# Hyena transforms handed over by halves of the frequencies, low parts of turned tiles ahead of the last taps

## The reference

```python
def long_conv(u, k):
    n = 2 * u.shape[1]
    uf = jnp.fft.rfft(u.astype(jnp.float32), n=n, axis=1)
    kf = jnp.fft.rfft(k, n=n, axis=0)
    return jnp.fft.irfft(uf * kf[None], n=n, axis=1)[:, :u.shape[1]].astype(u.dtype)

def hyena_mixer(a, ...):
    u = dwconv_centered(a @ in_w + in_b, conv_w, conv_b)
    x1, x2, v = jnp.split(u, 3, axis=-1)
    z = x1 * (long_conv(v, two_sided(...)) + v * bias[0])
    y = x2 * (long_conv(z, two_sided(...)) + z * bias[1])
    return y @ out_w + out_b
```

## Time and profile before

| | us |
|---|---|
| median of three runs | 2147.05 |
| lowest and highest | 2145.24, 2148.67 |
| the profiled execution | 2147.36 |
| its span, first to last instruction | 2145.5 |
| TensorE busy with matmuls | 2001.8 |
| VectorE busy | 1321.3 |
| ScalarE busy | 686.0 |
| GpSimd busy | 202.8 |

### The profile page before, as it was taken

How to read it: one execution, slowest core, us unless ns; L and a number is a source line. 1 busy time by engine, 2 the same in 40 slices (tenths; PEclk the granted TensorE clock), 3 DMA queues, 4 the chain that set the end, 5 groups by cost and what they waited for, 6 DMA issues and landing times. The chain is left out here.

```text
span 2145.5 us, 24954 instructions
## 1 busy us (share of the span) xinstructions
PE 2001.8 (93%) x10136; PEld 1672.0 (78%) x10136; DVE 1321.3 (62%) x1844; ACT 686.0 (32%) x913; POOL 202.8 (9%) x140
## 2 busy tenths in 40 slices
PE   5899999999989989999999999999899797698998
PEld 2688888878867868888887888888787784398998
DVE  6565546777857675554767565567765548845544
ACT  3422222232200232222224222222444335634442
POOL 1000000100023400000110000011000003340001
PEclk9999999999989999999999999999999898999999
DMA  8444435544520154442645444355432322444554
GB/s 322 152 159 155 137 106 183 165 139 135 179 76 1 41 165 148 139 155 83 201 153 171 138 152 143 104 173 165 147 118 89 118 84 74 123 133 152 186 155 141
DMA packets 274590, 298.25 MB, mean 139 GB/s; under 512 B 8912, under 2 KB 249136, under 8 KB 272688
## 3 DMA queue, kind: packets, MB, share of 16 engines
q1 hardware_dynamic: 270784, 285.44, 41.6%
q10 hardware_dynamic: 3696, 11.27, 1.4%
HBM read 290.31 MB, written 6.37 MB: 138 GB/s over the span
## 5 line engine op out<-in xcount | busy, mean ns | idle before, releaser
L1493 PE MATMUL banks<-xh,wh 128*128 128x512 f32 (+1 forms) x2120 | 782.3, 369 | 53.1 <-DVE xl L946 16.4
L1494 PE MATMUL banks<-xl,wh 128*128 128x512 f32 (+1 forms) x2120 | 777.0, 366 | 0.0
L1495 PE MATMUL banks<-xh,wl 128*128 128x512 f32 (+1 forms) x2120 | 776.4, 366 | 0.0
L883 DVE TENSOR_TENSOR wl<-raw,wh 128x2048 fp32r<-128x2048 f32 (+1 forms) x195 | 404.2, 2073 | 333.0 <-ACT wh L558 331.9
L558 ACT ACTIVATE wh<-raw 128x2048 fp32r<-128x2048 f32 (+1 forms) x201 | 349.6, 1739 | 644.6 <-PE banks L1495 562.9
L1493 PEld LDWEIGHTS banks<-xh,wh 128*128 128x128 f32 x2120 | 408.4, 193 | 124.5 <-issue 27.5
L1494 PEld LDWEIGHTS banks<-xl,wh 128*128 128x128 f32 x2120 | 408.4, 193 | 62.4
L1495 PEld LDWEIGHTS banks<-xh,wl 128*128 128x128 f32 x2120 | 407.8, 192 | 63.1
L1493 PE MATMUL banks<-gh,wh 128*128 128x512 f32 (+1 forms) x704 | 255.7, 363 | 2.9 <-DVE wl L883 1.6
L1494 PE MATMUL banks<-gl,wh 128*128 128x512 f32 (+1 forms) x704 | 255.2, 362 | 0.0
L1495 PE MATMUL banks<-gh,wl 128*128 128x512 f32 (+1 forms) x704 | 255.1, 362 | 0.0
(11 more groups left out here) (211 smaller groups left out, 1730.5 us busy)
## 6 DMA issues: line engine op xcount, KB each, us to landing
raw<-in_ffn_in SPq DMA_DIRECT2D x88, 1024.0 KB, 5.1
raw<-in_ffn_out SPq DMA_DIRECT2D x64, 704.0 KB, 4.8
ada_rawf<-in_ada_rest SPq DMA_DIRECT2D x60, 512.0 KB, 3.9
ada_rawo<-in_ada_rest SPq DMA_DIRECT2D x48, 512.0 KB, 4.0
raw<-in_mb_in_w SPq DMA_DIRECT2D x24, 1024.0 KB, 5.4
raw<-in_hy_in_w SPq DMA_DIRECT2D x12, 1024.0 KB, 5.2
afb<-decays SPq DMA_DIRECT2D x32, 256.0 KB, 3.1
raw<-in_mb_out_w SPq DMA_DIRECT2D x8, 1024.0 KB, 5.8
```

The costliest lines, as they stand in the source:

```text
L883: dve.tensor_tensor(wl[n_slot][:, 0:cols], raw[r_slot][:, 0:cols], wh[n_slot][:, 0:cols].bitcast(F32), ALU.subtract).then_inc(w_lo, 1)
L1493: pe.matmul(dst, h, x_hi, start=start, stop=False)
L1494: pe.matmul(dst, h, x_lo, start=False, stop=False)
L1495: return pe.matmul(dst, l_, x_hi, start=False, stop=stop)
```

## The change

1. The frequencies are taken in the order HALVES = (0, 2, 1, 3) by transform, products and sums. `transform` counts `fwd_mm` after each half of its four groups, and it waits for products by halves too: its first two groups for the first two products of the unit before, the other two for all four. `spectrum` waits for a half.
2. In the first transform the wait for emptied banks is spread: 22 evictions first (banks 0 and 1), then 23, 22 and 24 ahead of the groups on banks 2, 1 and 3.
3. ScalarE makes the high parts of the first two turned tiles ahead of the last two evictions of the input projection.
4. VectorE makes the low parts of the first four turned tiles ahead of the last two tiles' taps, and so ahead of its wait for `ksb`.

```diff
+        HALVES = (0, 2, 1, 3)
@@ ScalarE
+            def turned_hi(conv, j0, j1):
+                for j in range(j0, j1):
+                    act.wait_ge(vt_t, conv * 8 + j + 1)
+                    act.activation(xh[:, TURN[j], :], bank[turn_bank(conv, j)][:], ACT.Copy).then_inc(vt_hi, 1)
...
                     act.wait_ge(w_used, i * 2 + (HYIN.w + u + 1))
+                    if last and u == 1:
+                        turned_hi(0, 0, 2)
                     for s in range(2):
...
-            for conv in range(2):
-                for j, b in enumerate(TURN):
-                    act.wait_ge(vt_t, conv * 8 + j + 1)
-                    act.activation(xh[:, b, :], bank[turn_bank(conv, j)][:], ACT.Copy).then_inc(vt_hi, 1)
-            act.wait_ge(fwd_mm, 8)
+            turned_hi(0, 2, 8)
+            turned_hi(1, 0, 8)
+            act.wait_ge(fwd_mm, 16)
@@ VectorE
                     if u == 0:
                         ada_weigh(ADA_HY.load + i, ada_rawh, cb1, 0 if i else C_BASES["hy"])
+                    elif last:
+                        turned_lo(0, 0, 4)
                     for s in range(2):
...
-                for n in range(4):
+                for o, n in enumerate(HALVES):
...
-                    dve.wait_ge(fwd_mm, x + 1)
-                    c0 = x * 4 + n
+                    dve.wait_ge(fwd_mm, 2 * x + o // 2 + 1)
+                    c0 = x * 4 + o
                     if c0 >= 2:
                         dve.wait_ge(y_sum, c0 - 1)
-                    w0, w1 = tt[2 * (n % 2)], tt[2 * (n % 2) + 1]
+                    w0, w1 = tt[2 * (o % 2)], tt[2 * (o % 2) + 1]
...
-            turned_lo(0, 0, 4)
@@ GpSimd
-                for n in range(4):
-
-                    pool.wait_ge(cm_mul, x * 4 + n + 1)
-                    pool.tensor_tensor(prod[x % 2][:, n, :], tt[2 * (n % 2)][:], tt[2 * (n % 2) + 1][:],
+                for o, n in enumerate(HALVES):
+
+                    pool.wait_ge(cm_mul, x * 4 + o + 1)
+                    pool.tensor_tensor(prod[x % 2][:, n, :], tt[2 * (o % 2)][:], tt[2 * (o % 2) + 1][:],
@@ TensorE
-                if x:
-                    pe.wait_ge(cm_mul, 4 * x)
-                for ft in range(4):
+                for o, ft in enumerate(HALVES):
+                    if x and o % 2 == 0:
+                        pe.wait_ge(cm_mul, 4 * x - 2 + o)
+                    elif x == 0 and o:
+                        pe.wait_ge(z_free, HYIN.zf + 21 + ft)
                     for k in range(2):
...
-                ins.then_inc(fwd_mm, 1)
+                    if o % 2:
+                        ins.then_inc(fwd_mm, 1)
...
-            pe.wait_ge(z_free, HYIN.zf + 24)
+            pe.wait_ge(z_free, HYIN.zf + 22)
```

More of the change, by code:

```diff
@@ L1098, in _, with turned_lo @@
             norm("hy", 0, 3, HYIN)
+            def turned_lo(conv, j0, j1):
+                for j in range(j0, j1):
+                    b = TURN[j]
+                    dve.wait_ge(vt_hi, conv * 8 + j + 1)
+                    dve.tensor_tensor(xl[:, b, :], bank[turn_bank(conv, j)][:], xh[:, b, :].bitcast(F32),
+                                      ALU.subtract).then_inc(vt_lo, 1)
             def hy_in_pair(i, last):
```

## The result

The changed kernel takes 2129.45 us in the median of four runs (2125.97 to 2130.85), against 2147.86 for four runs of the kernel before (2145.24 to 2148.76). The ratio is 0.992, with a 95% interval of 0.9904 to 0.9937. The forecast was 2128.7 us, in 2125.5 to 2133.0. The profiled execution took 2130.85 us, with a span of 2129.1.

A forecast was written before the change was run, and what follows sets the result against it. TensorE, busy 93%, was taken as the bound, so only its stops and low clock pay. 9.2 + 2.46 + 0.45 + 5.44 + 1.44 = 19.0, less 0.7 for the clock, 18.3: forecast 2128.7 us, range 2125.5 to 2133.

The forecast's parts named there:

- One of the signs: In each unit: two products issued before its transform ends, which would show the forecast right.
- Part one: Entry of the first convolution: second transform starts 9.2 us earlier, and takes 2.46 us less if the clock holds.
- The clock term: Second transform of the first convolution: 0.7 us charged for a possible low clock, with ends 0 and 2.46.
- the 1.75 us stop: A TensorE stop in the kernel before that left the clock at 1.00, held nearest for the clock charge.
- Rival (1): Entry of the first convolution: clock falls in the short stop, costing 2.46 us; 2130.5 us, chance 0.22.
- Parts two to four: Between convolutions 0.45 us less, entry of the second convolution 5.44 less, exit at the last inverse transform 1.44 less.
- the thin cover: Exit: output weight's low part ends 0.8 to 2.6 us before TensorE's first matmul on it.
- rival (2): Exit: output weight late by up to 1.6 us, so 2130.3 us; chance 0.06.
- the four other terms: Gains beside the clock: 9.2 at first entry, 0.45 between convolutions, 5.44 at second entry, 1.44 us at exit.
- Rival (3): Both convolutions' entries: halves buy nothing, products slower while TensorE writes other banks; 2140.2 us, chance 0.06.
- Rival (4): Units: VectorE becomes the bound, slower overall beyond 15.5 us per unit; 2167 us at twice its time, chance 0.03.

The follow-up runs named there:

- The first kernel of the study: The changed kernel with high parts, low parts and last taps back in their old order, only the hand-over by halves kept; 2132.94 us, ratio 0.9936.
- the second: The changed kernel with products waiting for whole transforms and transforms for all four products, the early low parts kept; 2141.12 us, ratio 0.9971.
- the second trace: The full change run once more as control, nothing altered against the changed kernel; 2129.0 us, ratio 0.9914.

## Why the prediction was right

**What bounds, and where the halves pay.** As forecast: the stops at the two entries and at the exit are shorter or gone, and the steady units still take 12.36 us (621.29 - 608.93). The first kernel of the study shows that the halves take away the stops ahead of the two second transforms and the one at the exit, the second that without them these stops return. One of the signs came in part only: two products of each unit before its transform ends. In the first unit the products start at 599.20, after the transform has ended at 598.05, because the taps stand before them. There the halves pay only since the second transform asks for half of the products.

**Part one.** The first transform starts 2.16 us after the transposes (forecast 2.06), the second 11.46 (forecast 11.36). That the taps and the spread of ScalarE's order set the restart is shown by the two kernels that move them: 0.9 and 2.1 us earlier.

**The clock term was mis-sized.** I charged 0.7 us within 0 to 2.46. It measured 1.51, and 1.55 in the second trace. I held the 1.75 us stop to be the nearer row. The clock did come down, but only 1.5 us after the restart (at about 603.3, with the stop ended at 601.78), and it rose again at about 606.7. So the price is neither of those read off before, where the low clock was there from the first matmuls. My rows were also too few to order stops by their length: the trace before has one of 3.23 us behind which the clock stayed at 1.00, and the window shown for the 1.75 us stop covers the stop itself and not what came after it (there, too, 1.00). Rival (1) had the right fall, with too high a price. The rule of the Trainium skill, "TensorE: Matmul & The Clock Gate", Part 4: PE-mode transpose, which the prediction set beside it, does not give the reason: with transposes in the place of the idle time the clock holds.

**Parts two to four.** Between the convolutions 649.02 - 640.55 = 8.47 us (forecast 8.46). The entry of the second convolution 661.91 - 649.02 = 12.89 (forecast 13.04). The rest 700.44 - 661.91 = 38.53, against 717.67 - 677.80 = 39.87 before: 1.34 less (forecast 1.44). The output weight's low part, 3.39 us from 695.51, ended at 698.9, 1.7 us before TensorE wanted it; the thin cover held, and rival (2) did not come.

**The sum.** 18.3 less the 0.8 by which the clock cost more, and 0.1 net from the other terms, gives the 17.4 of the stage. The medians differ by 18.4, the two profiled executions by 16.5; what lies between is the spread of the parts outside of the stage. That the medians differ by just what I forecast is therefore luck, to about a microsecond; the mechanism and the four other terms are not.

**Rival (3)**, products of no use beside running transforms, is out: they keep their spacing of 0.6 us beside a running transform (618.77, 619.38, 619.97 and 620.57, with the transform from 615.64 to 621.29) as beside transposes and an idle engine (599.20, 599.81, 600.41, 601.00). **Rival (4)** put the point of no gain at 65% more of VectorE's work and units of 15.5 us. With the products doubled VectorE is busy for 14.39 us of the 14.80 us unit, 60% more than the 8.98 of the full change, and the kernel is already slower than before by 15 us. The mechanism exists, and it sets in earlier than I had reckoned, since I had counted units only and not the ends; the change itself is not near it.

## What to carry to other kernels

Handing over a stage by halves pays only where a pipeline fills or drains; between full units, where the bounding engine has no hole, it moves nothing. When two edits shorten the same chain, add up the chain and not the edits: here 15.0 and 6.5 us made 17.4. And when an engine starts late, look at what stands before that instruction in its queue and who needs it: the taps in front of the first product were not wanted until the second convolution, and a reordering that costs no instruction cut the stage by 2.5 to 3.7 us more, 1.5 of it by the clock.

## What the runs showed of the hardware

Transposes of 128 by 128 in fp32 kept TensorE's granted clock at 1.00 through 7 us of nothing else. A stop of 1.83 us behind transposes brought it to 0.50 for 3.4 us, beginning 1.4 to 1.5 us after work had started again, in both traces; one of 0.92 us at the same place did not, in one trace. A fall can therefore show up inside work that is already running, and its cause lies before it. The length of a stop does not settle the outcome: of two stops of 2.14 us in one trace the clock fell behind one only, and one stop of 3.23 us was followed by 1.00 in the kernel before and by 0.51 in the changed one. Filling the stop of 1.83 us with matmuls whose result nobody reads won 1.5 us of the stage. That the total gains as much can't be told from these medians.
